# A two-layer decoder trunk on one core: small constants packed into laid-out tables on ScalarE's queue, x loaded in four quarters, and a changed order of the first steps

## The reference

```
for l in (0, 1):
    h = rms(x, norm_mix[l])
    q, k, v = split(h @ w_in[l])               # 1024 x 3072; 16 heads of 64
    x += mix(q, k, v) @ w_out[l]               # 4 differential, 6 dilated, 6 MoBA heads,
                                               # q and k normed per head and rotated by position
    m = rms(mem, norm_mem[l])                  # 256 x 1024 memory rows
    x += memory_attention(rms(x, norm_cross[l]) @ w_mq[l], m @ w_mkv[l]) @ w_mo[l]
    x += swiglu(rms(x, norm_ffn[l]) @ w_gate_up[l]) @ w_down[l]
```

## Time and profile before

| | |
|---|---|
| median of 3 runs | 710.26 us (709.78 to 711.72) |
| span of the profiled execution | 707.8 us |
| PE busy | 691.5 us, 98% |
| DVE, ACT, POOL busy | 505.4, 392.9, 94.3 us |
| chain that ended last, shares | PE 82%, DVE 10%, ACT 4%, DMA 2% |

### The profile page before, as it was taken

The page is one execution under the profiler, slowest core; times in us unless marked ns, Lnnn a source line. Parts: engine busy times, 40 slices in busy tenths (PEclk is TensorE's granted clock), DMA queues, the critical chain, the costliest instruction groups (busy, mean ns, idle before and its releaser), DMA issues.

```text
span 707.8 us, 10791 instructions
## 1 busy us (share of the span) xinstructions
PE 691.5 (98%) x3794; PEld 571.6 (81%) x3794; DVE 505.4 (71%) x1012; ACT 392.9 (56%) x642; POOL 94.3 (13%) x92
## 2 busy tenths in 40 slices
PE   8999999999999999999999999999899999999997
PEld 7777776777988888888878777778788888888886
DVE  4898977576766666666579888775677666666665
ACT  6865776467544444444465658764764444444441
POOL 6331011217000000000032210202440000000000
PEclk9999999999999999999999999999999999999999
DMA  8945341244576666666546635113265666666631
GB/s 301 343 126 175 124 159 58 79 119 139 161 212 197 182 178 178 178 181 187 203 141 197 225 114 179 60 61 117 65 211 148 189 203 199 199 195 196 179 119 60
DMA packets 121216, 115.64 MB, mean 163 GB/s; under 512 B 3008, under 2 KB 95312, under 8 KB 121184
## 3 DMA queue, kind: packets, MB, share of 16 engines
q1 hardware_dynamic: 120224, 113.32, 52.1%
q0 software_dynamic: 384, 1.14, 0.5%
q10 hardware_dynamic: 576, 0.77, 0.3%
HBM read 114.17 MB, written 1.05 MB: 163 GB/s over the span
## 4 chain that ended last, share of the span: by engine, by line
PE 82%; DVE 10%; ACT 4%; DMA 2%; issue 1%; SPq 0%; POOL 0%; DVEq 0%; ACTq 0%
PE ps L1884 21%; PE ps L1515 16%; PE ps L1889 11%; PE ps L1924 5%; PE ps L1925 5%; PE ps L1926 5%; PE ps L1584 3%; PE ps L1907 3%; DVE wlo L907 3%; DMA raw<-in_w_in 2%; PE ps L1642 2%; PE ps L1654 2%; PE ps L1823 2%; PE ps L1690 1%; ACT sq L813 1%; PE ps L1438 1%
## 5 line engine op out<-in xcount | busy, mean ns | idle before, releaser
L907 DVE TENSOR_TENSOR wlo<-raw,whi 128x2048 fp32r<-128x2048 f32 (+1 forms) x96 | 214.1, 2246 | 40.4 <-ACT whi L604 39.0
L604 ACT ACTIVATE whi<-raw 128x2048 fp32r<-128x2048 f32 (+1 forms) x102 | 189.1, 1877 | 16.2 <-PE ps L1926 7.3
L1884 PE MATMUL ps<-both,whi 128*128 128x512 f32 x640 | 159.2, 391 | 0.0
L1884 PEld LDWEIGHTS ps<-both,whi 128*128 128x128 f32 x640 | 117.6, 188 | 22.7
L1515 PE MATMUL ps<-whi,both 128*128 128x512 f32 x384 | 100.5, 396 | 1.9 <-ACT whi L590 1.2
L855 ACT ACTIVATE qkv<-ps 128x512 f32<-128x512 f32 x44 | 26.4, 599 | 122.1 <-PE ps L1889 120.1
L1889 PEld LDWEIGHTS ps<-both,wlo 128*128 128x128 f32 x640 | 87.3, 190 | 6.2
L1889 PE MATMUL ps<-both,wlo 128*128 128x256 f32 x640 | 89.2, 282 | 0.0
L1515 PEld LDWEIGHTS ps<-whi,both 128*128 128x128 f32 x384 | 70.5, 188 | 18.4 <-issue 2.6
L1924 PE MATMUL ps<-whi,ahi 128*128 128x512 f32 x176 | 69.3, 393 | 1.7 <-DVE alo L1397 1.7
L1925 PE MATMUL ps<-wlo,ahi 128*128 128x512 f32 x176 | 69.0, 392 | 0.0
(11 more groups left out here) (211 smaller groups left out, 909.6 us busy)
## 6 DMA issues: line engine op xcount, KB each, us to landing
raw<-in_w_gate_up SPq DMA_DIRECT2D x88, 512.0 KB, 5.0
raw<-in_w_in SPq DMA_DIRECT2D x23, 1024.0 KB, 5.1
raw<-in_w_down SPq DMA_DIRECT2D x22, 1024.0 KB, 5.0
raw<-in_w_out SPq DMA_DIRECT2D x8, 1024.0 KB, 5.1
raw<-in_w_mkv SPq DMA_DIRECT2D x4, 1024.0 KB, 5.3
raw<-in_w_mq SPq DMA_DIRECT2D x4, 512.0 KB, 3.5
raw<-in_w_mo SPq DMA_DIRECT2D x2, 1024.0 KB, 5.0
xs<-in_x SPq DMA_DIRECT2D x2, 512.0 KB, 5.7
```

Of the source, the lines that this page charges most:

```text
L604: ins = act.activation(whi[s][:, cols], raw[s][:, cols], ACT.Copy)
L907: ins = dve.tensor_tensor(wlo[s][:, cols], raw[s][:, cols], hi, ALU.subtract)
L1884: pe.matmul(ps[:, bank, :], whi[s][:, a:a + P], both[:, :, k, :], start=(k == 0), stop=False)
```

## The change

The five small tables of the start become one, `starter`: the identity (128 columns), the norm gains (64), the frequencies (40) and the positions (2), laid out in DRAM as 234 columns for each of the 128 partitions, some 120 KB, loaded by the first instruction of ACT's queue. `g_rot` and `g_col` become `turn_gains`, 172 columns, laid out for all partitions and loaded on ACT's queue. POOL's queue issues none of the small loads any more, and its load of `mem` comes behind the root. The mask table (`table`, 384 KB) is issued later, at g = 14. x is loaded in four quarters of 256 KB in the order 0, 2, 1, 3; the PE transposes quarter 0 at the start and the others ahead of g = 2, 4 and 5. ACT rounds unit 1 ahead of the last quarter and sums the squares of both halves of x after it. The ones-products at the start are 6 in place of 8, and ACT makes a small copy of ones ahead of the first loaded data.

```diff
+FIRST_ORDER = (0, 2, 1, 3)
+FIRST_AT = (2, 4, 5)
+TABLE_AT = 14
-WARM = (8, 3)
+WARM = (6, 3)
...
 # SP
-            sp.dma_start(ident, consts["ident"]).then_inc(s_ident.sem, 16)
-            sp.dma_start(xs[:, 0, :], x_in[:, 0, :]).then_inc(s_x[0].sem, 16)
+            def x_quarter(q):
+                t, h = divmod(q, 2)
+                cols = slice(512 * h, 512 * h + 512)
+                sp.dma_start(xs[:, t, cols], x_in[:, t, cols]).then_inc(s_x[q].sem, 16)
+            x_quarter(FIRST_ORDER[0])
...
-                            sp.dma_start(xs[:, 1, :], x_in[:, 1, :]).then_inc(s_x[1].sem, 16)
+                            for q in FIRST_ORDER[1:]:
+                                x_quarter(q)
...
 # POOL
-            with nc.allow_non_contiguous_dma(reason="256 positions"):
-                pool.dma_start(pos_i[:], positions.rearrange("b (t p) -> p (b t)", p=P)).then_inc(s_pos.sem, 16)
-            pool.dma_start(g_rot[:].rearrange("p l e n -> p (l e n)"),
-                           gains["rot"].to_broadcast((P, DEPTH * 2 * NROT))).then_inc(s_rot.sem, 16)
-            pool.dma_start(g_col[:].rearrange("p l e n -> p (l e n)"), consts["g_col"]).then_inc(s_rot.sem, 16)
...
-                pool.wait_ge(s_pos.sem, 16)
-                pool.wait_ge(s_freq.sem, 16)
-                link(pool.tensor_copy(pos_f[:], pos_i[:]))
+                pool.wait_ge(s_starter.sem, 16)
+                link(pool.tensor_copy(pos_f[:], pos_i))
...
+                root(0, T)
                 if layer == 0:
                     pool.dma_start(mem_sb[:], mem_rows).then_inc(s_mem.sem, 16)
-                root(0, T)
...
 # ACT
-            act.dma_start(g_rows[:].rearrange("p l g k -> p (l g k)"), consts["g_rows"]).then_inc(s_rows.sem, 16)
-            act.dma_start(freqs[:], consts["freqs"]).then_inc(s_freq.sem, 16)
+            act.dma_start(starter[:], consts["starter"]).then_inc(s_starter.sem, 16)
+            act.wait_ge(s_ones.sem, 1)
+            act.activation(copy_warm[:], ones[:, 0:8], ACT.Copy)
...
+                if layer == 0:
+                    for n, q in enumerate(FIRST_ORDER):
+                        x_hi(0, X_MIX, q)
+                        if n == 0:
+                            split_hi(0, 0)
+                        if n == 2:
+                            split_hi(0, 1)
+                    act.dma_start(turn_gains[:], consts["turn_gains"]).then_inc(s_rot.sem, 16)
                     act.dma_start(small[:].rearrange("p l n -> p (l n)"),
                                   gains["small"].to_broadcast((P, DEPTH * N_SMALL))).then_inc(s_small.sem, 16)
-                    split_hi(0, 1)
-                for t in range(1 if layer == 0 else 0, T):
+                else:
+                    for q in range(2 * T):
+                        x_hi(layer, X_MIX, q)
+                for t in range(T):
                     squares_of_x(layer, 0, t)
                 split_hi(layer, 2)
...
+                    if layer == 0 and g == TABLE_AT:
+                        act.dma_start(table[:], consts["table"]).then_inc(s_table.sem, 16)
...
 # DVE
-            dve.wait_ge(s_rows.sem, 16)
+            dve.wait_ge(s_starter.sem, 16)
...
-                    x_lo(layer, X_MIX, 1)
-                for q in range(2, 4):
-                    x_lo(layer, X_MIX, q)
                 if layer == 0:
+                    x_lo(0, X_MIX, FIRST_ORDER[1])
+                    x_lo(0, X_MIX, FIRST_ORDER[2])
                     split_lo(0, 1)
+                    x_lo(0, X_MIX, FIRST_ORDER[3])
...
 # PE
-            pe.wait_ge(s_ident.sem, 16)
+            pe.wait_ge(s_starter.sem, 16)
-                for q in range(2):
+                for q in range(1 if layer == 0 else 2):
                     build_x(layer, X_MIX, q)
...
                 for g in range(LAST + 1):
-                    if g == (2, 3)[layer]:
+                    for n in range(1, 4):
+                        if layer == 0 and g == FIRST_AT[n - 1]:
+                            build_x(0, X_MIX, FIRST_ORDER[n])
+                    if layer and g == 3:
                         for q in range(2, 4):
                             build_x(layer, X_MIX, q)
```

More of the change, by code:

```diff
@@ L2090 @@
     rot = np.stack([rotated("qn"), rotated("kn")], axis=1)
[L2091 removed]
+    rot = np.tile(rot.reshape(1, -1), (P, 1))
     g_col = np.stack([unrotated("qn"), unrotated("kn")], axis=0)
     gains["small"] = put("small", np.concatenate([np.asarray(inputs[n]) for n in SMALL], axis=1).reshape(1, -1))
[L2094 to L2096 removed]
+    starter = [np.eye(P, dtype=np.float32), rows.transpose(3, 0, 1, 2).reshape(P, -1), freq_table(),
+               np.ascontiguousarray(positions, np.int32).view(np.float32)]
+    consts = {"starter": put("starter", np.concatenate(starter, axis=1)),
+              "turn_gains": put("turn_gains", np.concatenate([rot, g_col.transpose(2, 1, 0, 3).reshape(P, -1)], axis=1)),
+              "table": put("table", mask_table().reshape(P, -1))}
     out = nc.dram_tensor("out", (1, SEQ, D), F32, kind="ExternalOutput").ap()
[L2098 removed]
+    trunk(nc, x, mem, w, gains, consts, out)
     r = run_bass_kernel_spmd(nc, [arrays], core_ids=[0])
```

69 lines of the change are left out of this document (32 added, 37 removed).

## The result

| | before | changed |
|---|---|---|
| median, 21 runs each | 710.38 us | 711.55 us (from 710.95) |
| ratio, 95% interval | | 1.0018 (1.001 to 1.0025) |
| span of the profiled execution | 707.8 us | 710.7 us |
| the same execution's time | | 713.4 us |
| median span of the 20 executions measured with it | | 708.95 us |

Three executions of the kernel before (967 us) and one of the changed kernel (1368 us) were disturbed; the ratio leaves them out, and without them the medians are 710.3 and 711.54 us. The change costs 1.2 us, 0.18%: inside the 0.3% that I had set as what can be told, and inside my range, but not nothing, as the interval shows. The profiled execution is one of the long ones: fourteen of the twenty spans are 708.4 to 709.1 us, six are 710.1 to 710.7 us.

What follows compares the result with a forecast made beforehand. It took the chain of ACT and DVE up to S as the bound, not the PE. S moves 0.0 us, so a span of 707.8 us plus 2.0 to 3.9 us around it gave 710.2 us; range 708.4 to 711.9 us.

Steps and rivals of the forecast that it cites:

- What bounds the kernel: Before 42 us: any PE gain is waited away at 42.12 us unless the work of ACT and DVE comes earlier.
- S: Where ACT's first `chunk_out` and DVE's start on unit 3's low part stand, about 23.0 us; forecast at 23.05 us.
- the forecast wait of 1.8 us: PE's wait at 42.12 us, ahead of the first transposes of q and k, growing from 0.76 us.
- Rival 3: At 42 us: DVE has room, so the PE keeps its 1.05 us lead; 709.2 us, chance 0.15.
- The chain from `x_hi` of quarter 1 to S: ACT never idle from 12.4 us, units 1 and 2 with squares between, then DVE's low part; ends at 23.05 us.
- The start: First microseconds: transposes at 4.0 us, first `x_hi` done at 6.15 us, `x_lo` at 6.2 us instead of 7.69 us.
- rival 1: At DVE's `x_lo`: unit 0's second part lands no earlier, S 1.45 us later; 711.7 us, chance 0.14.
- Rival 4: From `x_lo` to S: the early start is nearly all gain, 1.45 us faster; 708.8 us, chance 0.15.
- Rival 2: At the first transposes and products: PE starts at a lower clock, costing 1.2 us; 711.4 us, chance 0.08.
- the sum: Whole kernel: S changes by 0.0 us, span 707.8 us, 2.0 to 3.9 us around it, median 710.2 us.
- The landing of mem: Load behind the root, issued at 20.8 us, landing at 30.0 us; PE may wait 1.6 us, costed at nothing.

Runs made afterwards that it cites:

- second profile: The changed kernel run again unedited and profiled: span 708.7 us, time 711.16 us.
- e3: The changed kernel with the first half's sum of squares put back behind `x_hi` of the second quarter: 710.54 us, ratio 1.0002.
- e7: The changed kernel with 8 ones-products, quarters transposed earlier (ahead of g = 2, 2, 4) and the first half's squares ahead of the second quarter: 707.88 us, ratio 0.9962.
- e9: The kernel before with `starter`, `turn_gains`, mem behind the root, `table` at g = 14 and the small ACT copy; halves, old order, 8 ones-products: 707.40 us, ratio 0.9962.
- e2: The changed kernel with 8 ones-products at the start instead of 6: 710.58 us, ratio 1.0000.
- e12: e7 with `starter` loaded in two transfers, identity and gains first: 708.03 us, ratio 0.9967.
- e8: The kernel before with only the four quarters of x and the new order; small loads and 8 ones-products as they were: 712.1 us, ratio 1.0025.
- e4: The kernel before with 6 ones-products at the start instead of 8: 711.32 us, ratio 1.0007.
- e1: The changed kernel run again unedited: 711.57 us, ratio 1.0011.
- e5: The kernel before with only `starter` and `turn_gains` in place of the small loads; mem ahead of the root, halves, old order, 8 ones-products: 708.44 us, ratio 0.9975.
- e10: The changed kernel with two more ones-products as the PE's last instructions: 711.03 us, ratio 1.0008.
- e6: The changed kernel with 6 ones-products at the start and 5 instead of 3 behind the first transposes: 710.25 us, ratio 1.0006.
- e11: e7 with 6 ones-products at the start and 5 behind the first transposes, instead of 8 and 3: 707.86 us, ratio 0.9961.
- f3: The changed kernel with four more ones-products as the PE's last instructions: 710.94 us, ratio 1.001.
- f2: The changed kernel with 10 ones-products at the start instead of 6: 711.47 us, ratio 1.0010.
- f1: The changed kernel with 7 ones-products at the start instead of 6: 711.54 us, ratio 1.0009.
- f4: e9 with 6 ones-products at the start instead of 8: 709.55 us, ratio 0.998.

## Why the prediction was right or wrong

**What bounds the kernel: right.** Whatever the PE won before 42 us it stood and waited there. From S to the transposes of q and k are 19.36 us in the second profile (43.29 - 23.93), 19.37 us in e3 and 19.38 us in e7; the forecast wait of 1.8 us was 1.72 us. That its size came out is in part luck: I had the PE there at 40.3 us and the wait end at 42.1 us, and they were 41.57 and 43.29 us, both 1.2 us late. Before, the PE was there at 41.36 us, so it has not gained a lead; S went back. Rival 3, by which the lead would be kept, fell. In e9 S is at 20.65 us and the transposes at 40.03 us, 19.38 us again: DVE's last `mlo` ends at 39.89 us, and the PE's own work ahead of them at about 40.0 us. The PE has no lead left there, so an earlier S alone should gain next to nothing more; that was not tried.

**The chain from `x_hi` of quarter 1 to S: right.** 12.4 to 23.05 us were forecast, 10.65 us; from 13.49 us to S at 23.93 us are 10.44 us, and from 15.44 us (ACT's `x_hi` in the profiled execution) to 25.88 us 10.44 us too. That the squares ahead of unit 2 cost what the early start gains was right too: e3 measures them at 0.95 us. I had both prices and took from their sum that the change is worth nothing. The experiments say more: the constants gain some 3 us (e9) and the quarters with their order lose it again (3.2 us from e9 to e2), most of it by the place of the transposes and of the squares (2.7 us from e7 to e2).

**The start: the terms were too small by 1.1 us.** `x_hi` of quarter 1 is at 13.49 us for 12.4 us, and with 0.2 us too much in the chain behind it S is at 23.93 us where 23.05 us was forecast. Three terms:
- "For the two I take 2.5 and 3.0 us after an issue at 0.74 us": `starter` landed 4.0 us after it, 3.8 to 4.6 us over the profiles, about or above my upper end of 3.9 us. The row nearest in bytes (`ident`, 1.9 us) misled. `freqs`, second on the same queue, had taken 3.9 us, but `g_rows`, first on it with 32 KB, 2.1 us; with e12, where 96 KB took 3.8 us, neither the queue nor the bytes explain it, and the cause stays open. The transposes start at 4.75 us, not 4.0, and `x_lo` at 6.62 us, not 6.2: 0.4 us.
- "DVE needs 3.75 us from the start of `x_lo` to the end of the low part of unit 0": 4.00 us (7.66 + 2.96 - 6.62), 0.25 us.
- I had let g = 3 follow g = 2 at once. It needs ACT's `x_hi` of the second quarter, done at 10.57 + 1.14 = 11.71 us, and starts at 11.85 us, 1.17 us after g = 2 (10.68 us) rather than 0.91. In the profiled execution the wait has a row, 0.39 us for ACT at 13.80 us. From the end of the low part of unit 0 to `x_hi` of quarter 1 it is 2.87 us (13.49 - 10.62) where I had 2.45: 0.4 us.

The first weights came later than I took them but earlier than before: DVE rounds the second part at 6.12 us, after a wait of 0.39 us for it (5.4 us was taken; 7.35 us before). It was done with it at 6.60 us and `x_hi` was done at 6.58 us, so `x_lo` at 6.62 us lost next to nothing by it. So rival 1 fell in the changed kernel, by a narrow margin; e8 shows it where the software queue's loads stay. Rival 4 fell as well: the squares ahead of unit 2, which I had set against it, cost 0.95 us in e3.

**Rival 2 came true in part.** In six of twenty executions the start is long. In the profiled one a product takes 0.77 to 0.80 us rather than 0.50 us until 10.6 us, and the start loses 2.0 us, where I had worked out 1.2 us. The granted clock of its two stretches reads 1.00 all the same:

```profile
5.00:8.00 3.00, 3.00 (x14) 2.66 (x13) 2.00 (x7) 1.85 (x6) 2.77 (x7) 1.00 1.02 358
8.00:11.00 3.00, 3.00 (x15) 2.77 (x15) 2.75 (x4) 0.43 (x1) 2.71 (x5) 1.00 1.01 384
```

The Trainium skill, TensorE: Matmul & The Clock Gate, Part 1, says that the array starts at half its clock until sustained work releases it. The record lengths fit that: four records of ones-products take 1.06 us at 7.48 us in the long start and 1.05 us in e4 where the granted clock reads 0.50, against 0.61 us at 1.00. The granted-clock column doesn't show the long start itself, so that the clock is its cause rests on these lengths. Spans longer than the rest of their kernel by some 0.5 us or more came in 0 of 12 executions of e1, 0 of 12 of e2, 0 of 8 of e5 and 0 of 6 of e7, in 2 of 12 of e3, 3 of 12 of e10, 5 of 11 of e6, 2 of 7 of e9, 1 of 6 of e11, 1 of 6 of e12 and 1 of 11 of f3: mostly with six ones-products first and a wait behind them, but not only, and not always with them. Beside that of the changed kernel only those of e6, e10 and e11 were profiled, and they show the long records; in e3, e9, e12 and f3 it is not shown that the long spans have this cause. They don't make the median of the changed kernel, since e1 has none and the same median.

**The step that failed** is in the sum: "The profiled span stays at 707.8 us, what lies around it at 2.0 to 3.9 us". The second half is the larger error. I had taken the time around the span for a constant because I had only one span and three times. Execution by execution it is 1.75 to 1.88 us before and 2.0 to 3.0 us after, and of the 1.2 us lost some 0.8 us lie there (medians 2.63 and 1.8 us; 1.0 us by e1's runs) and 0.35 us in the span, by the late start above. The sum set 2.4 us around a span of 707.8 us; the kernel before has 1.8 us around a median of 708.4 us. That the two made the right 710.2 us is luck: the span was of a short execution, and the difference to other runs' times took up the error. I had priced the two removed ones-products at their time in the span alone. The runs show that the step goes with them:
- 8 or 10 at the start, or 6 with two more behind the first transposes: 1.74 to 1.88 us in every execution (before, e2, e5, e6, e7, e8, e9, e11, e12, f2);
- 6 or 7 at the start: medians 2.53 to 2.80 us (changed kernel, e1, e3, e4, f1, f4), whatever the rest of the kernel;
- 6 at the start and 2 or 4 at the end: 1.97 to 1.98 us.

What it is that takes longer stays open. The products at the end act after the whole program, so it isn't the start of the work alone; the number of instruction packets goes with it, 18 wherever it is 1.8 us, and doesn't separate the other two. It may hang on the length of PE's program or on where its last part falls, but no row of a profile shows the time around the span, and I tried nothing that changes the length without a product.

**The landing of mem: right in its cost.** 30.0 us was the forecast by the row of before, nothing was the cost. It landed 7.0 us after its issue at 20.99 us, at 28 us, and the PE transposes it from 29.57 us on without a wait. What I missed is what later issues free: with mem behind the root and the mask table at g = 14, unit 4 is there when ACT wants it (a wait of 0.83 us in e5, none in e9).

## What to carry to other kernels

Price the parts of a change apart, and run them apart: here one part was worth 3 us and another took nearly all of it back, and the sum looked like a change without effect. Look for a point from which the rest takes the same time in every version, as S does here, and read each version by it. Compare time and span execution by execution before calling what lies around the span a constant; a few instructions more or less on one engine moved it by 1 us. Work on an engine off the critical path is free only where it stands: a sum of squares that filled an idle place cost its full 1 us when it was moved onto the chain.

## What the runs showed of the hardware that I had not expected

- The time around the span has steps: 1.8 us with 8 or 10 ones-products at the start, 2.5 to 2.8 us with 6 or 7, 1.8 us with 6 and two more behind the first transposes, 2.0 us with 6 and some at the end.
- A transfer of 117 KB as the first on ACT's queue took 3.8 to 4.6 us to land, longer than a quarter of x, 256 KB, at the least (3.6 us), and twice as long as `ident` had taken. With 96 KB it took as long (3.8 us, e12).
- Without the small loads on the software queue the DMA engines moved 412 rather than 203 GB/s between 5 and 8 us, at much the same busy share (1.06 against 0.91).
- The first products on the PE can take 0.77 us rather than 0.48 us until about 10 us in one execution and not in the next of the same kernel, at a granted clock of 1.00 in both; the lengths are those of a granted 0.50 (ones-products, 1.06 us in the one and 1.05 us in e4).
- After the PE had waited 2.09 us, at about 11 us, the granted clock fell from 1.00 to 0.50 (1.2 GHz), and it was back at 1.00 by 15 us (e4).
